# Column tiles and a new order in the recurrent stage, row groups at the head of the second expert loop, and one uninterrupted sum in the first modulation

## What is computed

```python
def first_block(x, c, w_ada, b_ada, ...):
    mod = jnp.einsum('bd,de->be', jax.nn.silu(c), w_ada[l]) + b_ada[l]
    sh_m, sc_m, gt_m, sh_f, sc_f, gt_f = jnp.split(mod[:, None, :], 6, axis=-1)
    u = layer_norm(x) * (1.0 + sc_m) + sh_m
    mix = hybrid_mixer(u, ...)          # gated linear recurrence and forgetting attention
    x = layer_norm(DEEPNORM_ALPHA * x + (1.0 + gt_m) * mix, ln1_g[l], ln1_b[l])
    ...                                 # experts, 2 groups of products

def second_block(x, c, ctx, c_ctx, w_mod, b_mod, g_pre_mix, ...):
    sh1, sc1, gt1, sh2, sc2, gt2 = jnp.split((silu_c @ w_mod[i] + b_mod[i])[:, None, :], 6, axis=-1)
    mod_c = jnp.split(silu_cc @ w_mod[i][:, :n_mod * D] + b_mod[i][:n_mod * D], n_mod)
    h = rmsnorm(x, g_pre_mix[i]) * (1 + sc1) + sh1
    ...
    f = moe_ffn(tokens, w_router[i], b_router[i], w_gu[i], b_gu[i], w_dn[i], b_dn[i])

def moe_ffn(h, w_router, b_router, w_gu, b_gu, w_dn, b_dn):   # 32 experts, 4 per token
    ...
        return act @ w_dn[e] + b_dn[e]
```

## Time and profile before

| | |
|---|---|
| three runs | 2774.55, 2779.63, 2781.0 us, median 2779.63 |
| the profiled execution | 2780.48 us, span of its records 2778.7 us |
| granted PE clock, mean over the span | 0.942 |
| PE busy | 2509.2 us, 90% |
| DVE busy | 2171.2 us, 78% |
| ACT busy | 1600.8 us, 58% |
| POOL busy | 473.3 us, 17% |
| place A | about 24 to 41 us |
| place B, the recurrent stage | about 168 to 248 us |
| place C | about 1462 to 1483 us |

### The profile page before, as it was taken

One profiled execution on the slowest core, in us unless ns is written; L12 is line 12 of the kernel. 1 busy time (PEld: TensorE's weight loads), 2 busy tenths in 40 slices (PEclk: granted clock), 3 DMA queues, 4 the chain that ended last, 5 costly groups with the idle time before them and its releaser, 6 DMA issues. The chain is left out here.

```text
span 2778.7 us, 35256 instructions
## 1 busy us (share of the span) xinstructions
PE 2509.2 (90%) x11844; PEld 2018.0 (73%) x11844; DVE 2171.2 (78%) x2098; ACT 1600.8 (58%) x1495; POOL 473.3 (17%) x330
## 2 busy tenths in 40 slices
PE   7987786999979997878968999999999999999994
PEld 6843665777768885767755888788888878888883
DVE  6777765999963426877666999999999999999995
ACT  3224634777745324555215777777777777777773
POOL 1212001222200000000011222222222222222220
PEclk9998977999989998989967999999999999999997
DMA  9765216999963420020226999999999999999995
GB/s 328 255 210 187 58 46 216 352 366 381 381 245 97 142 77 1 1 92 31 101 101 219 351 365 362 374 369 365 363 362 360 356 360 358 371 374 367 364 361 176
DMA packets 252415, 711.54 MB, mean 256 GB/s; under 512 B 35002, under 2 KB 68041, under 8 KB 250095
## 3 DMA queue, kind: packets, MB, share of 16 engines
q1 hardware_dynamic: 226132, 640.27, 62.8%
q0 software_dynamic: 22240, 59.81, 7.8%
q10 hardware_dynamic: 3968, 10.49, 1.0%
HBM read 691.55 MB, written 41.49 MB: 264 GB/s over the span
## 5 line engine op out<-in xcount | busy, mean ns | idle before, releaser
L51 PE MATMUL psum_all<-sb_ring_r,sb_arena_r 128*128 128x512 f32 (+1 forms) x2352 | 909.1, 387 | 0.0
L159 DVE TENSOR_TENSOR sb_ring_r<-sb_ring,sb_hi_ring_r 128x2048 fp32r<-128x2048 f32 x285 | 644.3, 2285 | 140.7 <-ACT sb_hi_ring_r L150 134.4
L159 DVE TENSOR_TENSOR sb_ring_r<-sb_ring,sb_arena_r 128x2048 fp32r<-128x2048 f32 x258 | 582.4, 2285 | 51.4 <-ACT sb_arena_r L150 51.2
L150 ACT ACTIVATE sb_arena_r<-sb_ring 128x2048 fp32r<-128x2048 f32 x258 | 485.1, 1911 | 216.6 <-DMA sb_ring<-in_w_gu_dram 206.7
L150 ACT ACTIVATE sb_hi_ring_r<-sb_ring 128x2048 fp32r<-128x2048 f32 x285 | 540.8, 1914 | 83.1 <-DMA sb_ring<-in_w_gu_dram 33.9
L51 PEld LDWEIGHTS psum_all<-sb_ring_r,sb_arena_r 128*128 128x128 f32 x2352 | 448.2, 191 | 90.3
L50 PE MATMUL psum_all<-sb_hi_ring_r,sb_arena_r 128*128 128x512 f32 (+1 forms) x1304 | 498.0, 382 | 15.3 <-DVE sb_ring_r L159 5.2
L52 PE MATMUL psum_all<-sb_hi_ring_r,sb_arena_r 128*128 128x512 f32 (+1 forms) x1304 | 493.6, 379 | 0.0
L50 PE MATMUL psum_all<-sb_arena_r 128*128 128x512 f32 x1064 | 430.5, 405 | 7.2 <-DVE sb_arena_r L2324 2.5
L52 PE MATMUL psum_all<-sb_arena_r 128*128 128x512 f32 x1080 | 427.9, 396 | 0.0
L50 PEld LDWEIGHTS psum_all<-sb_hi_ring_r,sb_arena_r 128*128 128x128 f32 x1304 | 248.3, 190 | 70.5 <-issue 10.2
(11 more groups left out here) (475 smaller groups left out, 3241.9 us busy)
## 6 DMA issues: line engine op xcount, KB each, us to landing
sb_ring<-in_w_gu_dram SPq DMA_DIRECT2D x272, 1024.0 KB, 7.0
sb_ring<-in_w_dn_dram SPq DMA_DIRECT2D x136, 1024.0 KB, 9.4
sb_ring<-in_w_e_gate_dram SPq DMA_DIRECT2D x36, 1024.0 KB, 7.8
sb_ring<-in_w_e_up_dram SPq DMA_DIRECT2D x36, 1024.0 KB, 7.8
sb_ring<-in_w_e_down_dram SPq DMA_DIRECT2D x36, 1024.0 KB, 7.2
sb_ring<-in_w_in_dram SPq DMA_DIRECT2D x27, 1024.0 KB, 5.8
sb_arena<-in_w_ada_dram POOLq DMA_DIRECT2D x32, 512.0 KB, 5.6
sb_ring<-in_w_mod_dram SPq DMA_DIRECT2D x16, 1024.0 KB, 5.0
```

Source lines behind the costliest of these rows:

```text
L51: eng.matmul(out, a[0], b[1], start=False, stop=False)
L150: act.activation(s.hi[c % len(s.hi)], s.raw[c % len(s.raw)], ACT.Copy).then_inc(s.hi_made, 1)
L159: dve.tensor_tensor(s.lo[c % len(s.lo)], s.raw[c % len(s.raw)], s.hi[c % len(s.hi)].bitcast(F32), ALU.subtract).then_inc(s.lo_made, 1)
```

## The change

It has three parts.

- A: in `first_in`, `put(0, "sh1", 0.0)` moves on DVE from between the scale's second and third accumulate to behind its last one.
- B: in `gates_and_lru`, piece b of a chunk now goes to PSUM partitions 32b and 32b + 1, and the bank is chosen by the half c. Two chunks stand before the gate products, in place of four. DVE multiplies the input gate with the convolved rows before the series, and the running sum and its splits move behind the recurrence's preparation; on ACT the same splits move behind the square root. ACT's two copies of 2 x 2048 become four of 2 x 1024. The attention stage's handling of these rows (loads, POOL's operations, stores) is spread over the four groups of partitions.
- C: in `experts`, the weights' copy is written four times, each to its own 32 partitions, `b_down` is loaded four times in `route`, the eight products run over four row groups into eight banks, with the half outermost, and the copies out of PSUM start behind all eight, with tile 3 first (its banks are those in which the first expert's rows are turned).

```diff
@@ first_in, DVE
             add_bias(0)
-            accumulate(1, 2)
-            accumulate(1, 3)
-            put(0, "sh1", 0.0)
-            for kd in range(4, KD - 1):
+            for kd in range(2, KD - 1):
                 accumulate(1, kd)
             add_bias(1)
             accumulate(1, KD - 1)
+            put(0, "sh1", 0.0)
             put(1, "sc1", 1.0)
@@ gates_and_lru, DVE
+            dve.wait_ge(s.gated, 2 * NJ)
+            dve.tensor_tensor(flat(ig), flat(ig), flat(xc), ALU.mult).then_inc(s.inner, 1)
             dve.wait_ge(s.exp, 1)
...
             link(dve.memset(t1, 1.0))
-            dve.tensor_tensor_scan(cum, t1, z, 0.0, ALU.mult, ALU.add).then_inc(s.summed, 1)
-            dve.wait_ge(s.part_hi, 1)
-            dve.tensor_tensor(t1, cum, fixed.parts[0:NF].bitcast(F32), ALU.subtract).then_inc(s.part_rest, 1)
-
-            dve.wait_ge(s.gated, 2 * NJ)
-            dve.tensor_tensor(flat(ig), flat(ig), flat(xc), ALU.mult).then_inc(s.inner, 1)
-            dve.wait_ge(s.part_hi, 3)
-            dve.tensor_tensor(fixed.parts[64:64 + NH], t1[64:64 + NH], fixed.third[64:64 + NH].bitcast(F32), ALU.subtract)
             dve.wait_ge(s.tanh, 1)
...
             dve.tensor_scalar(flat(gb), flat(gb), -1.0, None, ALU.mult).then_inc(s.variance, 1)
+            dve.tensor_tensor_scan(cum, t1, z, 0.0, ALU.mult, ALU.add).then_inc(s.summed, 1)
             dve.wait_ge(s.root, 1)
...
+            dve.wait_ge(s.part_hi, 1)
+            dve.tensor_tensor(t1, cum, fixed.parts[0:NF].bitcast(F32), ALU.subtract).then_inc(s.part_rest, 1)
             for j in range(NJ):
                 ins = dve.tensor_tensor_scan(gb[:, j, :], r[:, j, :], ig[:, j, :], 0.0, ALU.mult, ALU.add)
             link(ins)
+            dve.wait_ge(s.part_hi, 3)
+            dve.tensor_tensor(fixed.parts[64:64 + NH], t1[64:64 + NH], fixed.third[64:64 + NH].bitcast(F32), ALU.subtract)
@@ gates_and_lru, PE
-                    ins = pe.matmul(k.psum[32 * c:32 * c + 2, 4 + b, :], k.silu[:, KD + kd:KD + kd + KD + 1:KD],
+                    ins = pe.matmul(k.psum[32 * b:32 * b + 2, 4 + c, :], k.silu[:, KD + kd:KD + kd + KD + 1:KD],
...
-            for n in range(4):
+            for n in range(2):
                 modulate(n)
...
-            for n in range(4, len(mod_chunks)):
+            for n in range(2, len(mod_chunks)):
                 modulate(n)
@@ gates_and_lru, ACT: the five lines from wait_ge(s.summed, 1) to the copy to fixed.third move behind the square root
-            for c in range(2):
-                act.activation(mod_rows[32 * c:32 * c + 2], k.psum[32 * c:32 * c + 2, 4:8, :].rearrange("p b n -> p (b n)"),
+            for b in range(CHUNK // 512):
+                act.activation(mod_rows[32 * b:32 * b + 2], k.psum[32 * b:32 * b + 2, 4:6, :].rearrange("p c n -> p (c n)"),
                                ACT.Copy).then_inc(s.mod_put, 1)
@@ forgetting_attention, SP and POOL
-            sp.dma_start(bias_rows[0:2], b_mod[0:CHUNK].partition_broadcast(2)).then_inc(s.rows_loaded, 16)
-            sp.dma_start(bias_rows[32:33], a["b_mod_2"][:, CHUNK:2 * CHUNK]).then_inc(s.rows_loaded, 16)
+            for b in range(4):
+                for c in range(2):
+                    first = CHUNK * c + 512 * b
+                    sp.dma_start(bias_rows[32 * b:32 * b + 2, 512 * c:512 * c + 512],
+                                 b_mod[first:first + 512].partition_broadcast(2)).then_inc(s.rows_loaded, 16)
...
-            pool.tensor_tensor(mod_rows[32:33], mod_rows[32:33], bias_rows[32:33], ALU.add)
-            pool.tensor_tensor(mod_rows[0:2], mod_rows[0:2], bias_rows[0:2], ALU.add).then_inc(s.row, 1)
-            pool.wait_ge(s.row, 1)
-            pool.tensor_scalar(gained, gained, 1.0, None, ALU.add).then_inc(s.row, 1)
+            for b in range(4):
+                rows = slice(32 * b, 32 * b + 2)
+                pool.tensor_tensor(mod_rows[rows], mod_rows[rows], bias_rows[rows], ALU.add).then_inc(s.row, 1)
+            for b in (2, 3):
+                gained = mod_rows[32 * b:32 * b + 2, 0:512]
+                pool.wait_ge(s.row, b + 1)
+                pool.tensor_scalar(gained, gained, 1.0, None, ALU.add).then_inc(s.row, 1)
...
@@ route, SP
-                sp.dma_start(k.pair[0:m.experts].rearrange("p a d -> p (a d)"), b_down).then_inc(R.bias_landed, 16)
+                for t in range(TT):
+                    sp.dma_start(k.pair[32 * t:32 * t + m.experts].rearrange("p a d -> p (a d)"), b_down
+                                 ).then_inc(R.bias_landed, 16)
@@ experts, PE
-                pe.wait_ge(s.comb_read, 1)
-                pe.wait_ge(R.bias_landed, 48)
-                for t in range(TT):
-                    if t == 3:
-                        pe.wait_ge(s.y_made, 1)
-                    for hf in range(2):
-                        ins = pe.matmul(k.psum[:, 2 * (t % 3) + hf, :], comb_t[:, t * P:(t + 1) * P],
-                                        b_down[:, 512 * hf:512 * hf + 512], start=True, stop=True)
-                    ins.then_inc(s.y_summed, 1)
+                pe.wait_ge(s.comb_read, TT)
+                pe.wait_ge(R.bias_landed, 96)
+                for hf in range(2):
+                    for t in range(TT):
+                        rows = slice(32 * t, 32 * t + m.experts)
+                        ins = pe.matmul(k.psum[:, 2 * t + hf, :], comb_t[rows], b_down[rows, 512 * hf:512 * hf + 512],
+                                        start=True, stop=True)
+                ins.then_inc(s.y_summed, 1)
+            if biased:
+                pe.wait_ge(s.y_made, 1)
             turn_x(0, True)
@@ experts, ACT
-                act.activation(comb_t, k.psum[0:m.experts, YB, :], ACT.Copy).then_inc(s.comb_read, 1)
+                for t in range(TT):
+                    act.activation(comb_t[32 * t:32 * t + m.experts], k.psum[0:m.experts, YB, t * P:(t + 1) * P],
+                                   ACT.Copy).then_inc(s.comb_read, 1)
             make_hi(act, k, ss, 0)
             if biased:
-                for t in range(TT):
-                    act.wait_ge(s.y_summed, t + 1)
-                    act.activation(first_y[t], k.psum[:, 2 * (t % 3):2 * (t % 3) + 2, :].rearrange("p b n -> p (b n)"),
+                act.wait_ge(s.y_summed, 1)
+                for t in (3, 0, 1, 2):
+                    act.activation(first_y[t], k.psum[:, 2 * t:2 * t + 2, :].rearrange("p b n -> p (b n)"),
                                    ACT.Copy).then_inc(s.y_made, 1)
```

More of the change, by code:

```diff
@@ L898, in _ @@
             act.activation(flat(xc), flat(gb), ACT.Sqrt).then_inc(s.root, 1)
+            act.wait_ge(s.summed, 1)
+            act.wait_ge(s.fixed, 1)
+            act.activation(fixed.parts[0:NF], cum, ACT.Copy).then_inc(s.part_hi, 1)
+            act.wait_ge(s.part_rest, 1)
+            act.activation(fixed.parts[32:32 + NH], t1[32:32 + NH], ACT.Copy).then_inc(s.part_hi, 1)
+            act.activation(fixed.third[64:64 + NH], t1[64:64 + NH], ACT.Copy).then_inc(s.part_hi, 1)
             act.wait_ge(s.mod_used, len(mod_chunks))
-            for c in range(2):
-                act.activation(mod_rows[32 * c:32 * c + 2], k.psum[32 * c:32 * c + 2, 4:8, :].rearrange("p b n -> p (b n)"),
+            for b in range(CHUNK // 512):
+                act.activation(mod_rows[32 * b:32 * b + 2], k.psum[32 * b:32 * b + 2, 4:6, :].rearrange("p c n -> p (c n)"),
                                ACT.Copy).then_inc(s.mod_put, 1)
@@ L1179, in pool @@
         def pool(pool):
-            gained = mod_rows[0:2, D:2 * D]
-            pool.wait_ge(s.rows_loaded, 32)
-            pool.tensor_tensor(mod_rows[32:33], mod_rows[32:33], bias_rows[32:33], ALU.add)
-            pool.tensor_tensor(mod_rows[0:2], mod_rows[0:2], bias_rows[0:2], ALU.add).then_inc(s.row, 1)
-            pool.wait_ge(s.row, 1)
-            pool.tensor_scalar(gained, gained, 1.0, None, ALU.add).then_inc(s.row, 1)
-            pool.wait_ge(s.row, 2)
-            pool.wait_ge(s.gain_loaded, 16)
-            pool.tensor_tensor(gained, gained, bias_rows[0:2, D:2 * D], ALU.mult).then_inc(s.rows_made, 1)
+            pool.wait_ge(s.rows_loaded, 128)
+            for b in range(4):
+                rows = slice(32 * b, 32 * b + 2)
+                pool.tensor_tensor(mod_rows[rows], mod_rows[rows], bias_rows[rows], ALU.add).then_inc(s.row, 1)
+            for b in (2, 3):
+                gained = mod_rows[32 * b:32 * b + 2, 0:512]
+                pool.wait_ge(s.row, b + 1)
+                pool.tensor_scalar(gained, gained, 1.0, None, ALU.add).then_inc(s.row, 1)
+            pool.wait_ge(s.gain_loaded, 32)
+            for b in (2, 3):
+                gained = mod_rows[32 * b:32 * b + 2, 0:512]
+                pool.wait_ge(s.row, b + 3)
+                pool.tensor_tensor(gained, gained, bias_rows[32 * b:32 * b + 2, 0:512], ALU.mult).then_inc(s.rows_made, 1)
         def q_hi(act, h):
@@ L2004, in experts @@
         sel_up = [take(P, True) for _ in range(2)]
```

(6 more changed lines are left out.)

26 lines of the change are left out of this document (10 added, 16 removed).

## The result

| | before | after |
|---|---|---|
| median | 2777.86 us (4 runs, 2774.55 to 2781.0) | 2752.16 us (4 runs, 2751.66 to 2754.02) |
| ratio of medians | | 0.9909, 95% interval 0.9892 to 0.9926 |
| the profiled execution | 2780.48 us | 2751.66 us |

What follows compares the result with a forecast made beforehand. PE is busy 90% of the span, but three short places ahead of the second expert loop were taken to set the gain: 4.4 + 11.7 + 2.8 = 18.9 us off 2780.48, so 2761.6 us, range 2753 to 2771.

Steps and rivals of the forecast that it cites:

- the price of products on different tiles: Places B and C: products of two records overlap in pairs, 1.74 us per chunk in B, 7.9 us in C; chance 0.45.
- the term C: Head of the second expert loop: four row groups start the first expert's products 2.8 us sooner.
- the starting point: Whole kernel: gains were taken off the profiled execution's 2780.48 us, said to lie 0.85 above the median of three runs.
- the last chunk's landing: First modulation: the last chunk, landed at 29.99 by POOL's wait, limits DVE; the last accumulate ends at about 32.8.
- no chunk is waited for: First modulation: upper bound of edit A's gain, 5.3 us, with the scale's sum ready at 32.0.
- 4.4: First modulation: edit A's forecast gain in us, the scale's sum ending at 32.85 in place of 37.28.
- 11.7: Recurrent stage: edit B's forecast gain in us, DVE's own list ending the stage at 236.1 in place of 247.76.
- the attention stage: Behind the recurrent stage: gathering rows from four partition groups was taken to change 0 us, between -2 and +2.
- Full overlap: Rival for B and C: all four tiles run side by side, C gains 7.2 us, kernel 2757.2 us; chance 0.30.
- Late gates: Rival in the recurrent stage: half clock adds 7.1 us to the gate products, kernel 2768.2; chance 0.11, including similar losses.
- No overlap: Rival for B and C: tiles don't overlap, C loses 3.4 us, kernel 2779.8 us, no change; chance 0.09.
- drains at each change of tile: Rival for B and C: the array drains at each tile change, 0.16 us each, kernel 2791.2 us; chance 0.05.

Runs made afterwards that it cites:

- c_adjacent: The changed kernel with the two products of one row group next to each other at the head of the second expert loop (tile outermost, half inside): 2754.07 us.
- a_only: The kernel before with only edit A, the first modulation's scale added up in one go: 2773.65 us, ratio 0.9983.
- same: The kernel before run once more, unchanged: 2778.3 us over 11 runs, ratio 0.9997.
- c_only: The kernel before with only edit C, four row groups at the head of the second expert loop: 2771.10 us, ratio 0.9976.
- b_only: The kernel before with only edit B (column tiles, new order, two chunks ahead of the gates, attention stage's rows on four partition groups): 2765.98 us, ratio 0.9958.
- ahead4: The changed kernel with four chunks in place of two ahead of the gate products: 2752.72 us.

## Why the prediction was wrong

**The step that failed** is the price of products on different tiles: "the second record waits for the first and holds back the next product, which then starts beside it". The first half holds, the second doesn't (c_adjacent). Products on four groups cost the records of one group. In C that is 3.80 us in place of the 7.9 of nine steps, and the term C, -2.8, is -6.9 by the trace and -6.8 by the runs. That is 4.1 of the 6.8 us by which 18.9 fell short of 25.7; with 6.9 in the sum the forecast would have been 23.0 us, 2757.5. The 2.6 us of the starting point would by themselves have brought the measured time into the range too, but not the gain to its size. In B the same wrong price (1.74 us per chunk; 0.87 measured) was harmless by the traces: PE waits for a load ahead of each of the last ten chunks, and DVE ends the stage.

I had the right value as a rival at 0.30, and put the likeliest between two ends 3.5 us apart on a guess about the order of starts, which no row bore. The rival's 7.2 for C was 0.3 too much: the four copies of the weights add 0.54 us where I had 0.3, the sixteen records take 3.80 for 3.5, and from their end to the first expert's products it is 7.91 for 8.2. The figure of the Trainium skill that I weighed (TensorE: Matmul & The Clock Gate, Part 3: 3.07 times) was nearer than my own 1.8: four row groups gave 14.02 / 3.80 = 3.7 times.

**A: near in its number, wrong in its reason.** The forecast had the last chunk's landing as the limit, read from the moment when POOL goes on, and the last sum ready 2.8 us behind it. In the changed kernel POOL goes on at 30.91 and the sum is ready at 33.12, 2.2 behind it: DVE started on that chunk without waiting, so POOL's moment comes later than the landing. What holds is the bound "no chunk is waited for" plus the 0.22. The turns came at 33.17, for about 33, in an execution that ran 0.90 us late there, so this agreement is luck. From DVE's first addition to the scale until the first product L50 it takes 19.8 to 20.4 us in the six kernels without edit A and 15.1 to 15.3 in the eight with it: 4.9 us on average, near the bound of 5.3. The runs of a_only gave 4.3 (1.9 to 7.2), which holds both 4.4 and 4.9.

**B: right in its sum, less so in its parts.** The stage is 10.7 us shorter in the changed kernel (69.28 for 79.96) against 11.7. Of the missing 1.0, 0.76 is DVE's wait for the gates, which I had coming just in time. Their weights came when I said: the stage starts 3.33 us earlier here, and 184.99 + 3.33 = 188.3, for 188. But the products ran partly at the lower clock level, 8.55 us for 7.13. What I had put at 0, the attention stage, gained a little. All nine kernels with column tiles are 1.5 to 1.7 us further ahead of `same` some 40 us on than at the attention stage's start, and the four others without them stay within 0.2 us of it. POOL's timeline there, for the earlier trace rows, then the DVE scaling that had taken 4.00:

```profile
238.28 11.88 POOL L1186 TENSOR_TENSOR sb_arena<-sb_arena 2x1024 f32<-2x1024 f32 x4 [67.97 <-DMA sb_arena<-in_b_mod_dram]
```

```profile
242.18 1.85 DVE L1085 TENSOR_SCALAR sb_rows<-sb_rows,sb_small 128x128 f32<-128x128 f32 x1
```

The scaling takes less than half. That POOL's shorter pieces are the cause is argued from this and was not tried by itself.

**The rest.** By the traces A, B's stage, the attention stage and C make 4.9 + 10.7 + 1.6 + 6.9 = 24.1 us. The remaining 1.6 us to 25.7 is less than the measurement's uncertainty. The stretch between B and C, which holds the attention stage, takes 1204.34 to 1209.10 us in the nine kernels with column tiles and 1210.24 to 1213.59 in the five without: up to 4.8 us of spread for the same code. The nine lie 4.2 us lower on average (1206.9 for 1211.1), of which the attention stage explains 1.6. Compared operation by operation on ACT, the rest isn't spread over the stretch. It comes in jumps of 1.3 to 2.4 us at a few places, and kernels of both kinds show them: `before` and `same`, one kernel, differ above all by a jump of 2.4 at about 463 us on the clock of `same`, and c_only has the two near 850 and 1050 us that seven of the nine have (b_only and c_adjacent have at most half of the first). So the jumps don't need the column tiles. Why most kernels with them have these two, and what the jumps are, stays open.

**The rivals.** Full overlap came true in C and in B; its 2757.2 was 5.0 us too much: 2.6 from the starting point, and 2.4 of gain, as the attention stage (1.6), the rest (1.6) and A (0.5) gave more than it had and B's stage (1.0) and C (0.3) less. Late gates came true in small. No overlap and drains at each change of tile are refuted by 3.80 and 3.62 us. The rule of the Trainium skill on drains (TensorEngine Tiling (Array Packing), Key Properties) was to cost something at the two switches around the gate products: behind the gates it is 0.52 us from the last record's start to the next chunk's first, in ahead4 as in the kernel before, where records follow each other at 0.43. So this switch costs 0.09 us at most, and the change added nothing to it. The other switch lies behind a wait for loads and shows nothing.

## What to carry to other kernels

Small products that use 32 rows or 32 columns of the array are worth spreading over the four groups: the stretch costs about as much as the records on its fullest group. For row groups this held in both orders that were tried; for column groups only one order was. Before an order of work is tuned, find which engine ends the stage: here the new order alone gave nothing, and on top of the tiles 3.7 us. And where a price is unknown between two ends that rows give, a guess about the mechanism in between is no row; the range has to reach the cheap end together with what else may gain (here the attention stage, the starting point and the spread of runs), not stop in the middle of them.

## What the runs showed of the hardware that I had not expected

- Eight 32-bit products of two records each over four row groups: 3.80 us with neighbours on different groups, 3.82 with neighbours on the same group, 7.20 on two groups, 14.02 on one (all at the 1.2 GHz level). On four column groups: 0.87 us a chunk of four products for 3.47, at 2.4 GHz.
- Gate products behind an idle time of 1.16 to 1.84 us: 7.13 us; behind one of 2.71 to 4.34: 8.55 to 10.00, the first part at the 1.2 GHz level. The former also had four chunks ahead of them and the latter two. Single chunks behind idle times of 0.6 to 2.6 us ran at either level (1.04 or 1.89 us) or in between.
- Moving one square of 128x2048 from DVE to ACT brought DVE's 2.29 us down to an ACT operation of 1.92 that lay wholly in ACT's idle time; ACT's change of sign in the root's scale cost nothing (1.91 us with and without).
